# A two-block transformer kernel: attention probabilities scaled on ScalarE, chunks of a modulation product declared read one turn sooner, and weight copies placed ahead of waits

## The chip, the cores and the metric

The kernel runs on one core of a Trainium2 chip. The metric is the device time of one execution in microseconds (us); the time before is the median of three runs. A core has five engines that this text names: PE (TensorE, the matrix products), DVE (VectorE), ACT (ScalarE), POOL (GpSimd) and SP (SyncE, which here only issues transfers). Each engine works through its own list of instructions in order, and a semaphore holds one back until another engine has got far enough.

## The reference

What is computed is one token sequence of 256 rows by 1024 features that goes through a first block and then through two layers of a second kind, all in float32. Cut to what the change touches:

```python
# first block: m_lat = silu(c) @ w_ada + b_ada gives shifts, scales and gates
h = modulate(x, norm1_g, sh1, sc1)
z = h @ w_in + b_in                              # hyena input, q, k, v, gates
s_loc = einsum(q, k_window) * scale + rpb_bias   # 8 heads of 64, window over rows and columns
s_ctx = einsum(q, k_ctx) * scale
p = softmax(concat([s_loc, s_ctx]))              # 256 + 256 keys per query
y_na = (p @ [v_window; v_ctx]) @ w_na_out
y_hy = hyena(z) @ w_hy_out
x = x + g1 * ((sig_hy * y_hy + sig_na * y_na) @ w_out)
x = x + g2 * peer(modulate(x, norm2_g, sh2, sc2))
# then two layers
for l in range(2):
    a = dsa_attention(...)                       # 8 heads, softmax over 256 keys
    b = mamba2_branch(...)                       # state space product with decay exponentials
    x = x + (sigmoid(g_attn) * (a @ w_pa) + sigmoid(g_ssd) * (b @ w_ps)) @ w_o
    x = x + (silu(gate) * val) @ w_down          # gate, val = conv(rms_norm(x) @ w_up)
```

The modulation product `silu(c) @ w_ada` has one row only. Its later columns are computed not on PE but as dot products on DVE, from the transposed matrix `w_adaT`, of which each 512 KB chunk gives 128 of the columns.

## The kernel before, in words

**Products.** PE has no float32 product of full precision at full rate here; every product with weights is three products, w_hi·a_hi, w_lo·a_hi and w_hi·a_lo. ACT makes `w_hi` by copying a chunk out of the ring `wring` (L1440), POOL makes `w_lo` from it in two halves (L2809, L2811; for some matrices DVE does, L1876). The same is done with activations: ACT reads the high part from PSUM (`a_hi`, L1447) and DVE the low part (`a_lo`, L1953).

**The stream of weights.** SP issues the chunks in one fixed order, `wplan`, into a ring of six slots (L822 to L841). A chunk's transfer waits until the chunk six places ahead of it is no longer needed: for a product's chunk until its `w_lo` exists, for a chunk of `w_adaT` until its dot product has run. `weight_order` writes the plan and gives each chunk a turn, the place in the program at which the chunk is done with. The turns decide nothing about transfers; they decide where ACT, POOL and DVE put their copies in their own lists. `SplitStream.before(n)` issues every copy whose slot is done with by turn n, and it is called ahead of each wait for a filled bank (`wait_filled`), ahead of some reads (`wait_read`) and where `due` stands. `weights_upto` forces the copies up to a named chunk at once.

**The heads.** In the first block the eight attention heads go through a loop. For head h DVE adds the bias to the scores of two row tiles (L1960) and takes the maximum (L2259), adds the mask to the bias of the head after next (L1960), runs three modulation dots (`ada_dots`, L2241), takes the reciprocal of each row's sum (L2268) and multiplies the 128x512 exponentials by it (L2270), adds the gate bias in every other head (`gate_bias`, L2230), and at last writes the low part of the output of head h-1 (`na_low`, L1953). ACT takes the exponentials of head h with their sums (L1451), copies weights when they are due, reads the transposed probabilities of head h-1 out of PSUM (`nap`), and reads the high part of the output of head h-1 (`a_hi`, L1447). In the plan each head has two chunks of `w_in`, called W0 and W1 here, and then three of `w_adaT`, called A0, A1 and A2. With six slots and five chunks a head, W0 of head h+2 goes into the slot of A2 of head h, so its transfer waits until the last of the three dots of head h has run, and A0 of the next head waits until the `w_lo` of a W1 is made.

**Later places.** `exponentials` (L1730) is the softmax of the second block's attention, `decay` stands for the exponentials of the state space product (around L1785), `norm_tiles` and `tiles_turned` (L957) normalise and transpose the 256x1024 activations ahead of the feed-forward product.

## Time and profile before

| what | value |
|---|---|
| median of 3 runs | 2207.86 us (2206.05 to 2212.0) |
| profiled execution | 2212.09 us |
| its span | 2210.3 us |
| mean granted TensorE clock | 0.963 |
| PE busy | 1984.0 us, 90% of the span |
| DVE, ACT, POOL busy | 1377.4, 1002.8, 1048.6 us |
| memory read | 531.49 MB, 241 GB/s over the span |

The span runs from the first to the last instruction in the trace; what the profiled execution takes beyond it, 1.8 us, lies around it. PE at 90% says that most of the time a faster kernel would need less PE work or less waiting by PE; the places where PE is not busy are spread over few stages. The heads loop lies between 211 and 299 us, the second block begins past 1000 us, and its two layers repeat each other.

### The profile page before, as it was taken

The page shows a single profiled execution, that of the slowest core. Times are in us where ns is not written, and L with a number is a line of the kernel's source. Part 1 is how long each engine was busy: PE and PEld are TensorE (multiplying, and loading weights), DVE is VectorE, ACT ScalarE, POOL GpSimd, SP SyncE. Part 2 cuts the span into 40 slices and gives each one's busy share as a digit, 9 for nine tenths or more (in the row PEclk, how much of TensorE's full clock was granted, in tenths as well). Part 3 has the DMA queues.
Part 4 walks back from the last instruction along what each step waited for, and adds up shares of the span by engine and source line. Part 5 has one row for each costly group of instructions (what it writes and reads, how often), then busy time and mean ns, then how long its engine had stood idle before and what let it go on. Part 6 is the DMA issues. An engine that isn't in the chain of part 4 may idle for free.

```text
span 2210.3 us, 27141 instructions
## 1 busy us (share of the span) xinstructions
PE 1984.0 (90%) x9640; PEld 1469.2 (66%) x9640; DVE 1377.4 (62%) x2782; ACT 1002.8 (45%) x1836; POOL 1048.6 (47%) x840
## 2 busy tenths in 40 slices
PE   7999968987877787777999999999999999998998
PEld 1777756943323333333599777889989977777998
DVE  3768955486666676665457754167763775326776
ACT  1623435332222212212445687455564567845555
POOL 2362657764444444443387757900028865692000
PEclk9999979999898989999999999999999999999999
DMA  9242765699999999999655444545555534454553
GB/s 350 68 138 82 253 222 174 211 421 421 422 422 421 421 421 422 421 422 421 229 178 172 136 162 159 173 157 187 187 156 189 181 124 155 160 180 163 191 182 114
DMA packets 111447, 534.40 MB, mean 242 GB/s; under 512 B 12496, under 2 KB 12880, under 8 KB 77904
## 3 DMA queue, kind: packets, MB, share of 16 engines
q1 hardware_dynamic: 67104, 244.72, 33.1%
q0 software_dynamic: 38720, 275.96, 30.4%
q10 hardware_dynamic: 5488, 11.98, 1.7%
q8 instruction: 77, 1.26, 0.2%
q14 instruction: 58, 0.48, 0.1%
HBM read 531.49 MB, written 1.11 MB: 241 GB/s over the span
## 4 chain that ended last, share of the span: by engine, by line
PE 59%; DMA 22%; DVE 6%; ACT 6%; issue 3%; POOL 3%; ACTq 0%; POOLq 0%; DVEq 0%; SPq 0%
PE psum L877 57%; DMA pair_rows<-in_peer_uv,arena 11%; DMA arena<-in_peer_uv,arena 6%; DMA wring<-in_peer_uv,arena 3%; PE psum L945 2%; ACT w_hi L1440 2%; POOL w_lo L2811 2%; POOL w_lo L2809 1%; ACT arena L1451 1%; ACT arena L1785 1%; DVE arena L2551 1%; DMA wring<-in_w_in_hy 1%; DMA wring<-in_w_ada 0%; ACT arena L1730 0%; DVE arena L2567 0%
## 5 line engine op out<-in xcount | busy, mean ns | idle before, releaser
L2809 POOL TENSOR_TENSOR w_lo<-wring,w_hi 128x512 fp32r<-128x512 f32 x280 | 382.4, 1366 | 543.8 <-ACT w_hi L1440 535.5
L1440 ACT ACTIVATE w_hi<-wring 128x1024 fp32r<-128x1024 f32 (+1 forms) x414 | 433.7, 1054 | 334.4 <-PE psum L877 313.0
L877 PE MATMUL psum<-w_hi,a_hi 128*128 128x512 f32 (+1 forms) x1056 | 425.1, 403 | 44.8 <-POOL w_lo L2811 15.2
L877 PE MATMUL psum<-w_lo,a_hi 128*128 128x512 f32 (+1 forms) x1056 | 412.9, 391 | 0.0
L877 PE MATMUL psum<-w_hi,a_lo 128*128 128x512 f32 (+1 forms) x1056 | 412.3, 390 | 0.0
L877 PE MATMUL psum<-arena 128*128 128x512 f32 (+7 forms) x1142 | 336.3, 451 | 65.2 <-ACT arena L1658 50.7
L2811 POOL TENSOR_TENSOR w_lo<-wring,w_hi 128x512 fp32r<-128x512 f32 x280 | 394.8, 1410 | 0.0
L877 PE MATMUL psum<-a_hi,w_hi 128*128 128x256 f32 x1312 | 376.7, 287 | 4.1 <-DVE a_lo L1930 2.3
L877 PE MATMUL psum<-a_hi,w_lo 128*128 128x256 f32 x1312 | 372.0, 284 | 0.0
L877 PE MATMUL psum<-a_lo,w_hi 128*128 128x256 f32 x1312 | 371.9, 283 | 0.0
L877 PEld LDWEIGHTS psum<-arena 128*128 128x128 f32 (+2 forms) x1142 | 186.0, 198 | 198.0 <-issue 126.6
L877 PE MATMUL psum<-pair_rows,arena 128*128 128x512 f32 x512 | 247.2, 631 | 55.3 <-ACT arena L1658 55.3
L877 PEld LDWEIGHTS psum<-w_hi,a_hi 128*128 128x128 f32 x1056 | 201.4, 191 | 99.0 <-POOL w_lo L2811 18.0
L877 PEld LDWEIGHTS psum<-a_hi,w_hi 128*128 128x128 f32 x1312 | 252.2, 192 | 6.8 <-POOL w_lo L2811 3.0
L877 PEld LDWEIGHTS psum<-a_lo,w_hi 128*128 128x128 f32 x1312 | 252.5, 192 | 0.7
L877 PEld LDWEIGHTS psum<-a_hi,w_lo 128*128 128x128 f32 x1312 | 252.3, 192 | 0.0
L877 PEld LDWEIGHTS psum<-pair_rows,arena 128*128 128x128 f32 x512 | 100.4, 201 | 195.9 <-issue 118.0
L877 PEld LDWEIGHTS psum<-w_lo,a_hi 128*128 128x128 f32 x1056 | 201.7, 191 | 42.2 <-issue 3.9
L877 PEld LDWEIGHTS psum<-w_hi,a_lo 128*128 128x128 f32 x1056 | 201.4, 191 | 42.2
L2853 POOL DMA_INDIRECT pair_rows<-in_peer_uv,arena x128 | 137.3, 1072 | 162.8 <-PE psum L877 153.5
L1876 DVE TENSOR_TENSOR w_lo<-wring,w_hi 128x1024 fp32r<-128x1024 f32 x134 | 164.0, 1224 | 62.6 <-ACT w_hi L1440 59.1
L1653 ACT ACTIVATE arena<-arena 128x4 f32<-128x4 f32 (+2 forms) x69 | 14.3, 207 | 333.9 <-DVE arena L2428 333.9
(261 smaller groups left out, 2393.7 us busy)
## 6 DMA issues: line engine op xcount, KB each, us to landing
wring<-in_w_up SPq DMA_DIRECT2D x88, 512.0 KB, 3.3
wring<-in_w_xbc SPq DMA_DIRECT2D x48, 512.0 KB, 3.3
wring<-in_w_dn SPq DMA_DIRECT2D x44, 512.0 KB, 3.3
wring<-in_w_adaT SPq DMA_DIRECT2D x32, 512.0 KB, 4.3
wring<-in_w_qkv SPq DMA_DIRECT2D x32, 512.0 KB, 3.6
wring<-in_w_z SPq DMA_DIRECT2D x32, 512.0 KB, 3.2
wring<-in_w_g SPq DMA_DIRECT2D x32, 512.0 KB, 3.3
wring<-in_w_ps SPq DMA_DIRECT2D x32, 512.0 KB, 3.3
```

What stands on the lines that cost most here:

```text
L877: mm = lambda o, a, b, start, stop: nc.tensor.matmul(o, a, b, start=start, stop=stop, skip_group_check=True)
L945: m = nc.tensor.transpose(o[0:s.shape[-1], j * n:(j + 1) * n], s, ident[0:n, 0:n])
L1440: a.reaches(A(w_hi[:, n % SPLIT_RING, 0:width], wring[:, c % RING, 0:width], ACT.Copy), hi_ready, n + 1)
L1451: a.reaches(A(out_, in_, func, **kw), *read_value(name, i))
L1653: a.reaches(A(pact[:, cols_q], pdot[:, cols_q], ACT.Gelu), S("gelu_ready"), q + 1)
L1785: a.done(A(Lm[:, i % 2, (4 * half + j) * P:(4 * half + j + 1) * P], rows[:, j * P:(j + 1) * P], ACT.Relu, bias=acs_s[:, h:h + 1], scale=-1.0))
L1876: v.reaches(T.tensor_tensor(w_lo[:, r, 0:width], wring[:, c % RING, 0:width], w_hi[:, r, 0:width].bitcast(F32), ALU.subtract), *low_done(n))
L2551: ins = T.scalar_tensor_tensor(out=sc, in0=bank(L + "is", b_)[:, at * n_keys:(at + 1) * n_keys], scalar=wi[:, h:h + 1], in1=sc if h else c ...
L2809: nc.gpsimd.tensor_tensor(w_lo[:, r, 0:half], wring[:, c % RING, 0:half], w_hi[:, r, 0:half].bitcast(F32), ALU.subtract)
L2811: nc.gpsimd.tensor_tensor(w_lo[:, r, half:width], wring[:, c % RING, half:width], w_hi[:, r, half:width].bitcast(F32), ALU.subtract).then_ ...
L2853: pool.indirect_dma_start(out=pair(n), out_offset=None, in_=d["peer_uv"], in_offset=bass.IndirectOffsetOnAxis(ap=pidx[:, g, j:j + 1], axis ...
```

## The change

The change has five parts.

- The exponentials of a head are multiplied by the reciprocal of their sum on ACT (`Copy` with `scale=ainv`, sixteen of 128x512) and no longer on DVE. DVE makes the two reciprocals ahead of the three dots of the head, raises the new semaphore `na_inverse`, and has no multiplication left there. 
- In `weight_order` the turn of a `w_adaT` chunk of head h is `nao(h-1)` and no longer the turn after it.
- `tiles_turned` opens its eight PSUM banks one by one, each ahead of its first transpose, and not all eight ahead of the first.
- ACT's weight copies are forced earlier at four places: w_out 7 ahead of the first read of the output product, the second copy of `w2_z` ahead of the wait for the softmax maximum of the second row tile, `w2_o` 7 ahead of the reads of its product; and `w2_g` 5 moves to behind an `Exp`.
- POOL waits for `modulated_lo` and no longer for `tile_scaled` ahead of the low part of w_pq 1.

```diff
--- before.py
+++ after.py
@@ -381,7 +381,7 @@
             kp, c = 2 * ((h - 1) % 2) + k, (h - 1) // 2
             done = turn[("nap", 2 * h - 2)] if kp < 2 else turn[("gate", 2 * c)] if kp == 2 else turn[("gate", 2 * c + 1)] + 1
             w.append(("w_in", None, 12 + 4 * c + kp, CHUNK, done, kp == 3, True))
-        w.extend(("w_adaT", None, DOTS_PER_HEAD * (h - 1) + i, CHUNK, turn[("nao", h - 1)] + 1, True, False)
+        w.extend(("w_adaT", None, DOTS_PER_HEAD * (h - 1) + i, CHUNK, turn[("nao", h - 1)], True, False)
                  for i in range(DOTS_PER_HEAD))
     at = len(w)
     rows("w_hy_out", "mix", 2, two, 2)
@@ -949,9 +949,11 @@
 
         def tiles_turned(name, n):
 
-            o = [open_(name, k) for k in range(KD)]
+            o = []
             for t in range(TT):
                 for k in range(KD):
+                    if not t:
+                        o.append(open_(name, k))
                     if k % 4 == 0:
                         pe.wait_ge(S("tile_scaled"), 4 * n + 2 * t + k // 4 + 1)
                     m = nc.tensor.transpose(o[k][:, tile(t)], xs[:, t, tile(k)], ident)
@@ -1585,6 +1587,11 @@
                     read_out("nas", 2 * h + t, nap[h % 2][:, t, :], bank("nas", 2 * h + t), ACT.Exp,
                              bias=amax[:, 2 * h + t:2 * h + t + 1],
                              accum_out=asum[:, 2 * h + t:2 * h + t + 1])
+                for t in range(TT):
+                    i = 2 * h + t
+                    act.wait_ge(S("na_inverse"), i + 1)
+                    a.reaches(A(nap[h % 2][:, t, :], nap[h % 2][:, t, :], ACT.Copy, scale=ainv[:, i:i + 1]),
+                             S("na_prob"), i + 1)
             if h == 0:
                 act.wait_ge(S("c_row_in"), 16)
                 a.reaches(A(dve_junk[:], dve_junk[:], ACT.Silu), S("c_row_ready"), 1)
@@ -1604,6 +1611,8 @@
         for n in range(2):
             read_out("gb", n, G[:, 0, 512 * n:512 * n + 512], bank("gb", n))
         def first_half(i):
+            if i == 0:
+                weights_upto(act, "w_out", None, 7)
             due(act, "wout", i)
             wait_read(act, "wout", i)
 
@@ -1723,6 +1732,8 @@
 
             def exponentials(t, first):
                 n_keys = P * (t + 1)
+                if t:
+                    weights_upto(act, "w2_z", l, first + 1)
                 act.wait_ge(S("max2"), TT * l + t + 1)
                 for h in range(H2):
                     if h in (2, 5):
@@ -1787,10 +1798,12 @@
                     a.settle()
                     if i < SSD_G * TT - 1:
                         act.dma_start(rows, decay_rows(l, i + 1, half)).then_inc(S(f"decay_rows_in{half}"), 16)
-                    if i:
+                    if i and (i, half) != (1, 1):
                         ahead = 2 * i + 2 + half
                         weights_upto(act, *(("w2_g", l, ahead) if ahead < 16 else ("w2_pa", l, ahead - 16)))
                 a.reaches(A(Lm[:, i % 2, :], Lm[:, i % 2, :], ACT.Exp, scale=-1.0), S("decay_exp"), 8 * l + i + 1)
+                if i == 1:
+                    weights_upto(act, "w2_g", l, 5)
                 for g_ in range(SSD_G if i == 0 else 0):
                     read_out(L + "st", g_, st[:, g_, :], bank(L + "st", g_))
                 for n in (i - 1, i) if c else ():
@@ -1823,7 +1836,12 @@
                     weights_upto(act, *(("w2_o", l, 4) if k else ("w2_ps", l, 14)))
                 read_high(L + "mT", k, a_hi[:, k, :], bank(L + "mT", k)[:, 0:SEQ])
 
-            norm_tiles(1 + 2 * l, range(4), lambda i: wait_read(act, L + "wo", i))
+            def half_read(i):
+                if i == 0:
+                    weights_upto(act, "w2_o", l, 7)
+                wait_read(act, L + "wo", i)
+
+            norm_tiles(1 + 2 * l, range(4), half_read)
             scaled_high(L + "fT", KD, f"ffnw{l}")
             def glu_high(c):
                 for m_ in range(2):
@@ -2260,15 +2278,12 @@
                          S("na_max"), i + 1)
             if 0 < h < NA_HEADS - 1:
                 masked_bias(h + 1)
-            if h:
-                ada_dots(DOTS_PER_HEAD * (h - 1), DOTS_PER_HEAD * h)
             for t in range(TT):
                 i = 2 * h + t
                 wait_read(dve, "nas", i)
-                v.done(T.reciprocal(ainv[:, i:i + 1], asum[:, i:i + 1]))
-                v.settle()
-                v.reaches(T.tensor_scalar(nap[h % 2][:, t, :], nap[h % 2][:, t, :], ainv[:, i:i + 1], None, ALU.mult),
-                         S("na_prob"), i + 1)
+                v.reaches(T.reciprocal(ainv[:, i:i + 1], asum[:, i:i + 1]), S("na_inverse"), i + 1)
+            if h:
+                ada_dots(DOTS_PER_HEAD * (h - 1), DOTS_PER_HEAD * h)
             if h:
                 if h % 2 == 0:
                     gate_bias(h // 2 - 1)
@@ -2802,7 +2817,7 @@
             pool.wait_ge(hi_ready, n + 1)
             width, r = wplan[c][3], n % SPLIT_RING
             if c == chunk_at[("w_pq", None, 1)]:
-                pool.wait_ge(S("tile_scaled"), 4)
+                pool.wait_ge(S("modulated_lo"), 2 * KD + 1)
             if second_block + 2 <= c < second_block + SPLIT_RING:
                 pool.wait_ge(S("pair_used"), split_freed((SPLIT_RING + r) * CHUNK))
             half = width // 2
```

Rows of the engines' lists, as written out by the two programs. `w_hi<-wring` is a weight copy, and `weights_in2` the arrival of the chunk in ring slot 2. First ACT's list in the heads loop before, from the exponentials of one head:

```order
L1451 ACTIVATE arena,small_values<-psum,small_values 128x512 [waits psum_filled,na_max] x2
L1440 ACTIVATE w_hi<-wring 128x1024 [waits weights_used,weights_in2,psum_filled]
L1440 ACTIVATE w_hi<-wring 128x1024 [waits weights_used,weights_in3]
L1451 ACTIVATE arena<-psum 128x4x128 [waits psum_filled] x2
L1447 ACTIVATE a_hi<-psum 64x256 [waits psum_filled]
```

The same stretch of ACT's list after, from the reads of one head to those of the next:

```order
L1453 ACTIVATE arena<-psum 128x4x128 [waits psum_filled] x2
L1442 ACTIVATE w_hi<-wring 128x1024 [waits weights_used,weights_in2]
L1449 ACTIVATE a_hi<-psum 64x256 [waits psum_filled]
L1453 ACTIVATE arena,small_values<-psum,small_values 128x512 [waits psum_filled,na_max] x2
L1593 ACTIVATE arena<-arena,small_values 128x512 [waits na_inverse] x2
L1442 ACTIVATE w_hi<-wring 128x1024 [waits weights_used,weights_in3,psum_filled]
L1453 ACTIVATE arena<-psum 128x4x128 [waits psum_filled] x2
L1442 ACTIVATE w_hi<-wring 128x1024 [waits weights_used,weights_in1]
L1449 ACTIVATE a_hi<-psum 64x256 [waits psum_filled]
```

The copy of the slot 2 chunk (W0) has moved from behind the next head's exponentials to ahead of `a_hi` of this head, and there are two scalings behind the exponentials.

DVE's list in one head before, from the mask of the bias; ISA is the dot product and, with 128x1, the read of its sum:

```order
L1960 TENSOR_TENSOR arena<-arena 128x512 [waits rpb_in0]
L2241 ISA wring,small_values<-wring,dve_junk 128x1024 [waits weights_in0,c_row_ready]
L2241 ISA small_values 128x1
L2241 ISA wring,small_values<-wring,dve_junk 128x1024 [waits weights_in1]
L2241 ISA small_values 128x1
L2241 ISA wring,small_values<-wring,dve_junk 128x1024 [waits weights_in2]
L2241 ISA small_values 128x1
L2268 RECIPROCAL small_values<-small_values 128x1 [waits bank_read4]
L2270 TENSOR_SCALAR arena<-arena,small_values 128x512 [waits vector_steps]
L2268 RECIPROCAL small_values<-small_values 128x1 [waits bank_read5]
L2270 TENSOR_SCALAR arena<-arena,small_values 128x512 [waits vector_steps]
L1953 TENSOR_TENSOR a_lo<-psum,a_hi 64x256 [waits read_high,psum_filled]
```

The same head in DVE's list after:

```order
L1978 TENSOR_TENSOR arena<-arena 128x512 [waits rpb_in0]
L2284 RECIPROCAL small_values<-small_values 128x1 [waits bank_read4]
L2284 RECIPROCAL small_values<-small_values 128x1 [waits bank_read5]
L2259 ISA wring,small_values<-wring,dve_junk 128x1024 [waits weights_in0,c_row_ready]
L2259 ISA small_values 128x1
L2259 ISA wring,small_values<-wring,dve_junk 128x1024 [waits weights_in1]
L2259 ISA small_values 128x1
L2259 ISA wring,small_values<-wring,dve_junk 128x1024 [waits weights_in2]
L2259 ISA small_values 128x1
L1971 TENSOR_TENSOR a_lo<-psum,a_hi 64x256 [waits read_high,psum_filled]
```

The reciprocals, which wait for both exponentials (`bank_read4`, `bank_read5`), now stand ahead of the dots, and the two multiplications are gone.

## Rows read from the trace of the kernel before

**Rows 1.** the page: busy time by engine

```profile
PE 1984.0 (90%) x9640; PEld 1469.2 (66%) x9640; DVE 1377.4 (62%) x2782; ACT 1002.8 (45%) x1836; POOL 1048.6 (47%) x840
```

**Rows 2.** windows of two heads: PE, PEld, DVE, ACT, POOL busy; clock; DMA; GB/s

```profile
236.90:248.60 11.70, 11.70 (x49) 9.40 (x49) 10.45 (x16) 4.54 (x8) 7.17 (x5) 0.86 0.71 236
248.60:261.50 12.90, 10.49 (x50) 8.21 (x48) 11.71 (x19) 5.18 (x10) 8.31 (x6) 1.00 0.68 239
```

**Rows 3.** waits of PE, 211 to 299 us

```profile
PE psum L877 <- DVE arena L2230: 7.7, 3, 2.8
```

**Rows 4.** DVE in the heads: start, duration, instruction, count

```profile
224.76 0.41 DVE L1953 TENSOR_TENSOR a_lo<-psum,a_hi 64x256 fp32r<-64x256 f32 x1
...
249.41 0.42 DVE L1953 TENSOR_TENSOR a_lo<-psum,a_hi 64x256 fp32r<-64x256 f32 x1 [1.35 <-ACT a_hi L1447]
...
252.87 1.22 DVE L2241 CUSTOM_DVE_ANT_0 wring<-wring,dve_junk 128x1024 f32<-128x1024 f32 x1
...
255.15 2.28 DVE L2241 CUSTOM_DVE_ANT_0 wring<-wring,dve_junk 128x1024 f32<-128x1024 f32 x1
...
260.17 1.27 DVE L2230 TENSOR_TENSOR arena<-psum,arena 128x512 f32<-128x512 f32 x2
261.48 0.43 DVE L1953 TENSOR_TENSOR a_lo<-psum,a_hi 64x256 fp32r<-64x256 f32 x1
...
296.06 0.42 DVE L1953 TENSOR_TENSOR a_lo<-psum,a_hi 64x256 fp32r<-64x256 f32 x1 [1.20 <-ACT a_hi L1447]
```

**Rows 5.** ACT in the same head

```profile
248.93 0.38 ACT L1447 ACTIVATE a_hi<-psum 64x256 fp32r<-64x256 f32 x1 [3.20 <-PE psum L877]
...
252.97 0.19 ACT L1451 ACTIVATION_READ_ACCUMULATOR arena<-psum,small_values 128x1 f32 x1
253.06 1.99 ACT L1440 ACTIVATE w_hi<-wring 128x1024 fp32r<-128x1024 f32 x2
...
259.12 0.38 ACT L1447 ACTIVATE a_hi<-psum 64x256 fp32r<-64x256 f32 x1 [3.09 <-PE psum L877]
```

**Rows 6.** POOL in the same head

```profile
252.65 0.55 POOL L2823 DMA_DIRECT2D arena<-in_rpb  x1 [3.46 <-DVE small_values L2259]
254.20 2.15 POOL L2809 TENSOR_TENSOR w_lo<-wring,w_hi 128x512 fp32r<-128x512 f32 x1 [1.00 <-ACT w_hi L1440]
```

**Rows 7.** SP's queue: the transfers of W0 and W1 for head h+2

```profile
257.47 1.44 SPq L838 DMA_DIRECT2D wring<-in_w_in  x2
```

**Rows 8.** that transfer, and the first (222.04 us): size, us to landing

```profile
wring<-in_w_in SPq DMA_DIRECT2D x1, 512.0 KB, 3.7
...
wring<-in_w_in SPq DMA_DIRECT2D x1, 512.0 KB, 5.9
```

**Rows 9.** dots and multiplications: ns min/median/max, first and last start

```profile
L2241 DVE CUSTOM_DVE_ANT_0 wring<-wring,dve_junk x32: 1208/1222/2309, 218.5 to 351.6; 128x1024 f32<-128x1024 f32 x32
L2270 DVE TENSOR_SCALAR arena<-arena,small_values x16: 487/1294/1318, 214.0 to 293.6; 128x512 f32<-128x512 f32 x16
...
L1814 ACT ACTIVATE arena<-arena,small_values x16: 704/709/725, 1361.2 to 1930.1; 128x512 f32<-128x512 f32 x16
```

**Rows 10.** windows behind the last head

```profile
297.00:326.00 29.00, 13.96 (x58) 11.03 (x56) 13.48 (x21) 11.67 (x18) 18.59 (x12) 0.76 0.59 202
```

**Rows 11.** waits of PE, 1240 to 1300 us

```profile
PE psum L877 <- POOL w_lo L2811: 2.1, 1, 2.1
```

**Rows 12.** the window behind that wait

```profile
1260.00:1264.60 4.60, 4.60 (x14) 3.62 (x15) 2.08 (x1) 3.93 (x6) 4.25 (x3) 0.63 0.40 123
```

**Rows 13.** waits of PE at the feed-forward transposes, 1436 to 1456 us

```profile
PE psum L957 <- DVE arena L1904: 3.6, 1, 3.6
PE psum L877 <- POOL w_lo L2811: 1.1, 1, 1.1
```

**Rows 14.** DVE behind the modulated transposes of the first block

```profile
381.47 1.38 DVE L1930 TENSOR_TENSOR a_lo<-arena,a_hi 128x256 fp32r<-128x256 f32 x1
...
383.22 0.41 DVE L1930 TENSOR_TENSOR a_lo<-psum,a_hi 128x256 fp32r<-128x256 f32 x1
```

## The prediction

> **What bounds the kernel now.** I read the page's busy times first. PE is busy for 1984.0 of 2210.3 us [rows 1], so time can only go or come in the stages where PE waits. The windows show one such stage, the heads loop: one head takes 11.70 us with PE busy throughout at a granted clock of 0.86, the next 12.90 us with PE busy for 10.49 [rows 2]. The waits name the reason for the second kind: three stalls, 7.7 us together, on DVE's gate bias [rows 3]. That stall is no separate item. Read DVE's rows in order: the low part of a head's output, `a_lo`, starts at 249.41 and 261.48, and over six heads from 224.76 to 296.06 [rows 4]. (296.06 - 224.76) / 6 = 11.88 us is the period of the loop, and whatever makes DVE write `a_lo` later moves everything behind it, since the next head's score additions stand behind it on DVE.
>
> What lies in one period? From `a_lo` at 249.41, taken as zero: additions and maxima, the dots from +3.46 to +7.96 (252.87, then 1.15 apart, the third 2.28 long) [rows 4], two multiplications of 1.29 [rows 9] with their reciprocals, the gate bias at +10.76 and `a_lo` again at +12.07 [rows 4]. ACT has its exponentials' sums by +3.75, makes two weight copies in 1.99, and reads `a_hi` at 259.12, when PE has the product [rows 5]. SP issues W0 of head h+2 at 257.47, 0.1 after the last dot, because it goes into that dot's ring slot [rows 7]; it lands 3.7 us later, at 261.2 [rows 8]. Before, that landing is in nobody's way: the copy of W0 stands behind the next head's exponentials.
>
> **The change part by part.** *The new turn.* This edit is one number in `weight_order`, and it is the one that decides. The copy of W0 of head h+2 now stands in ACT's list ahead of `a_hi` of the same head. ACT is in order, so `a_hi` waits for the landing; DVE's `a_lo` waits for `a_hi`; the next head's additions, exponentials and dots wait for `a_lo`; and the next W0 is issued only behind those dots. The chain closes: dots, transfer, copy, `a_hi`, `a_lo`, additions, exponentials, dots. A transfer that was hidden becomes a link of the loop.
>
> *The reciprocals and multiplications.* Two multiplications leave DVE, 2 x 1.29 = 2.6 us a head [rows 9]. ACT's own scaling has no row; the nearest is its other 128x512 scaling from SBUF, 0.71 us [rows 9], so 1.4 a head, between 0.5 (what the quickest multiplication took on DVE) and 1.05 each (half of a double copy is 1.0 [rows 5]). ACT is idle for 3.09 us ahead of `a_hi` [rows 5], so this is hidden: nothing. In exchange the reciprocals now wait for both exponentials, whose sums are there at +3.75, so the first dot starts at about +3.95 in place of +3.46: +0.5. The gate bias (2.5 us) runs on DVE right behind the dots, while W0 is on its way (3.7 us), and costs nothing; its stall on PE is taken over by the wait for `a_hi`.
>
> *The new period.* Dots from +3.95, each 1.15 apart: end at +7.4. Then 0.1 issue, 3.7 landing, 1.0 copy and 0.4 for `a_hi` [rows 5, 7, 8]: 5.2. That makes 12.6 with three quick dots. A dot beside POOL's work takes 2.28 in place of 1.2 [rows 4], +1.1 each: 13.7, 14.8 and 15.9 with one, two and three slow ones. Before, only the third was slow, because POOL began its low part at 254.20, after ACT's copy, behind the bias transfer of 252.65 [rows 6]. Now W0's high part was made a head earlier, so POOL can begin at about +3.8, right behind that transfer and ahead of the first dot. I take two slow dots: 14.8. Six periods: (14.8 - 11.88) x 6 = +17.5; ends +4.3 and +24.1.
>
> The Trainium skill, "SBUF — State Buffer", section "Terms", says that DVE and GpSimd arbitrate for a port pair that is held exclusively for a whole instruction, the loser blocking. The lengths in rows 4 and 6 (a dot of 2.28, a low half of 2.15 against 1.37 on average) fit that rule; by it alone all three dots could alternate with POOL's halves, and the sum would take 15.9 for the period.
>
> *The first head.* The first W0 is issued at 222.04 and lands after 5.9 [rows 8]. With 0.5 for the reciprocals, 1.0 and 0.4, `a_lo` starts at 229.8 in place of 224.76 [rows 4]: +5.1.
>
> *Behind the last head.* From 297 to 326 PE is busy for 13.96 of 29 us and POOL for 18.59 [rows 10]: PE there waits for weight copies. One copy is already made when the loop ends, and transfers have had longer: I give back 4, between 0 and 8 (what two more chunks of copy and low part, 1.0 + 2.8 each, could be worth). The heads together: 17.5 + 5.1 - 4 = +18.6.
>
> *Copies ahead of waits.* At the second softmax of each layer PE stalls 2.1 us on a low part [rows 11], because ACT's copy for it stands behind the exponentials; the next 4.60 us run at a clock of 0.63, near the lower level of 1.2 GHz [rows 12], which costs about 4.60 x 0.37 = 1.7. The copy now stands ahead of that wait and pushes the exponentials by 1.0. I take 2.1 + 1.7 - 1.0 = 2.8 a layer, 5.6 for two; ends 0 (the softmax is late by as much) and 7.6. At the feed-forward transposes PE waits 1.1 for a low part [rows 13]; the earlier w2_o copy takes it: 2 x 1.1 = 2.2, ends 0 and 2.2. The 3.6 us wait of the transposes themselves is for DVE's data [rows 13], and opening banks one by one doesn't bring that sooner: nothing, at most some tenths. The copies of w_out 7 and w2_g 5 change places with neighbours while PE has work: nothing, within 1 either way.
>
> *POOL's wait.* The low part of w_pq 1 now begins after the modulated low parts; before, one of these was 1.38 long beside POOL and its like 0.41 [rows 14]: -0.9.
>
> **Sum.** +18.6 - 5.6 - 2.2 - 0.9 = +9.9 us. Against the profiled execution, 2212.1, that is 2222.0; the median of the runs is 4.2 lower than that execution, so the forecast is **2218**.
>
> **The rivals.**
> *One slow dot, as before.* The period is 13.7, (13.7 - 11.88) x 6 = +10.9, and the whole +10.9 + 5.1 - 4 - 8.7 = +3.3: 2211. For it: in before only one of three was slow. Against: POOL's low part is ready sooner. 0.2.
> *The full alternation of dots and halves* (the reading that the page's rule gives): 15.9, +24.1 + 5.1 - 4 - 8.7 = +16.5: 2224. For it: the lengths fit. Against: POOL has four halves of some 1.4 to do, and the bias transfer ahead of them. 0.15.
> *The late copies give nothing,* since the softmax or the data is late anyway: +18.6 - 0.9 = +17.7: 2226. For it: PE's wait on DVE of 3.6 right beside the 1.1 [rows 13]. 0.1.
> *The other side: PE bounds the heads.* In the head from 236.90, PE was busy to the end [rows 2] and ACT read `a_hi` at 248.93, when PE had it [rows 5]. If W0 lands by the time PE has the head's product, the copy ahead of `a_hi` costs 1.0 at most, and with 2.6 us off DVE the loop goes at PE's pace, 10.5 a head: (11.88 - 10.5) x 6 = -8.3, with the late copies -17: 2191. It decides from the point where the last dot ends 5.2 us ahead of that product. For it: the 2.6 us are real. Against: the dots start later, not sooner, and the sum from +3.95 to `a_lo` has no PE in it. 0.1.
> The main case has 0.45; its own range is 2213 to 2223.
>
> **How the numbers follow.** A measurement of this kernel can tell 0.3%, 6.6 us, from no change: the bounds are 2201 and 2214.5. Slower: of the main case 0.37, the full alternation 0.15, no gain later 0.1: 0.62. Same: 0.08 of the main case and 0.17 of the one slow dot: 0.25. Faster: PE's pace 0.1 and 0.03 of the one slow dot: 0.13. The range 2203 to 2228 leaves out PE's pace and the far end of the two dear cases.
>
> **What would show it.** The period of `a_lo` on DVE between the second and the eighth head: near 14.8 if right, 12 or less if the loop argument is wrong. ACT's weight copy ahead of `a_hi` should have idle time ahead of it that ends with a transfer of w_in, some 2 to 3 us in each head, and `a_hi` none that ends with PE. Two of three dots should be 2 us or longer. PE's stall on the gate bias should be gone and a longer one, on `a_lo` or `a_hi`, stand in its place. At the second softmax the stall on POOL's low part should be gone with the clock at full level behind it. If W0 is found landed before the copy gets to it in most heads, the forecast is wrong.

## The result, and the profile after

The changed kernel takes 2243.94 us (median of 4 runs, 2243.19 to 2244.54); the kernel before, beside it, 2207.63. The ratio is 1.0161, 95% interval 1.0143 to 1.0179: 36 us slower. The forecast was 2218, with a range that ended at 2228. The direction and the loop were as foretold; what one turn of the loop costs was not.

The profiled execution's span is 2242.7 us against 2210.3, 32.4 more. The page has the same number of matmuls, 18.8 us more of PE busy time and none more on DVE. The mean granted clock is 0.953 and was 0.963; in the six turns of the heads it lies between 0.65 and 0.96, before between 0.85 and 1.00, and the 0.65 belongs to the turn from 268.87 on, just ahead of which PE had waited 4.7 us. So part of the loss shows as longer matmuls, the rest, 13.6 us, as idle time of PE:

```profile
PE 2002.8 (89%) x9640; PEld 1482.2 (66%) x9640; DVE 1377.2 (61%) x2766; ACT 1012.0 (45%) x1852; POOL 1032.0 (46%) x840
```

The same matmul can be found in both traces, since PE's order is the same but for where banks are opened; the difference of its two starts says how late the changed kernel is at that point. First the changed kernel's PE at the output product of the first block and at the first product behind the modulated transposes; the instructions answering to them in the kernel before start at 326.29 and 382.99:

```profile
361.70 0.76 PE L877 MATMUL psum<-w_hi,a_hi 128*128 128x512 f32 x1 [11.31 <-DVE arena L2309]
...
417.35 0.55 PE L877 MATMUL psum<-a_hi,w_hi 128*128 128x256 f32 x1 [0.78 <-DVE a_lo L1948]
```

| stretch | forecast | measured in the traces |
|---|---|---|
| ahead of the heads | 0 | +1.1 |
| first head (to the first `a_lo`, 232.08 against 224.76) | +5.1 | +6.2 |
| six periods | +17.5 | +34.2 |
| last heads to the output product | -4 | -6.1 |
| behind the modulated transposes | -0.9 | -1.1 |
| all later stages | -7.8 | -1.9 |
| sum | +9.9 | +32.4 |

The sum is 32.4 and not 36 because the profiled execution of the kernel before was 4.5 us above its median and that of the changed kernel 0.6. The +1.1 ahead of the heads has arisen before 100 us, where nothing was edited; at that point the profiled executions of the twelve runs lie between 0.0 and 3.6 us behind the kernel before. Differences of that size between two whole traces can't be put down to an edit.

Now one turn of the loop. DVE, with the columns start, duration, instruction, count (the rows answer to [rows 4]):

```profile
232.08 0.42 DVE L1971 TENSOR_TENSOR a_lo<-psum,a_hi 64x256 fp32r<-64x256 f32 x1 [5.15 <-ACT a_hi L1449]
...
250.34 0.43 DVE L1971 TENSOR_TENSOR a_lo<-psum,a_hi 64x256 fp32r<-64x256 f32 x1 [4.90 <-ACT a_hi L1449]
...
254.26 5.95 DVE L2259 CUSTOM_DVE_ANT_0 wring<-wring,dve_junk 128x1024 f32<-128x1024 f32 x1
...
260.14 1.22 DVE L2259 CUSTOM_DVE_ANT_0 wring<-wring,dve_junk 128x1024 f32<-128x1024 f32 x1
...
261.28 1.21 DVE L2259 CUSTOM_DVE_ANT_0 wring<-wring,dve_junk 128x1024 f32<-128x1024 f32 x1
...
268.87 0.42 DVE L1971 TENSOR_TENSOR a_lo<-psum,a_hi 64x256 fp32r<-64x256 f32 x1 [6.36 <-ACT a_hi L1449]
...
337.61 0.42 DVE L1971 TENSOR_TENSOR a_lo<-psum,a_hi 64x256 fp32r<-64x256 f32 x1 [7.21 <-ACT a_hi L1449]
```

(337.61 - 232.08) / 6 = 17.59 us is the period, and the turn shown takes 18.53, against 11.88 before and 14.8 in the forecast. The dots run from +3.92 to +12.15 and no longer to +8.0, and it is the first of them that is long. POOL in that stretch answers to [rows 6]:

```profile
253.59 0.55 POOL L2838 DMA_DIRECT2D arena<-in_rpb  x1 [12.74 <-DVE small_values L2277]
254.16 1.29 POOL L2824 TENSOR_TENSOR w_lo<-wring,w_hi 128x512 fp32r<-128x512 f32 x1
255.39 1.29 POOL L2826 TENSOR_TENSOR w_lo<-wring,w_hi 128x512 fp32r<-128x512 f32 x1
256.63 1.27 POOL L2824 TENSOR_TENSOR w_lo<-wring,w_hi 128x512 fp32r<-128x512 f32 x1
257.85 1.27 POOL L2826 TENSOR_TENSOR w_lo<-wring,w_hi 128x512 fp32r<-128x512 f32 x1
```

The first dot starts 0.1 us behind the first of four low halves, and ends 1.1 us behind the last of them. The halves themselves are at their quick length of 1.27 to 1.29. SP and ACT then show the transfer and what waits for it (to [rows 5, 7]):

```profile
260.24 1.47 SPq L838 DMA_DIRECT2D wring<-in_w_adaT  x2
262.53 0.80 SPq L838 DMA_DIRECT2D wring<-in_w_in  x2
```

```profile
267.44 1.06 ACT L1442 ACTIVATE w_hi<-wring 128x1024 fp32r<-128x1024 f32 x1 [10.19 <-DMA wring<-in_w_in]
268.40 0.36 ACT L1449 ACTIVATE a_hi<-psum 64x256 fp32r<-64x256 f32 x1
```

W0 is issued as the last dot ends, ACT's copy starts 4.91 us later (the landing took 3.7 before [rows 8]), and the copy ahead of `a_hi` has waited 10.19 us. ACT's waits over all heads, in total, times and longest, name the transfer six times:

```profile
ACT w_hi L1442 <- DMA wring<-in_w_in: 53.1, 6, 10.3
```

The dots and the scalings on ACT, in ns (to [rows 9]): the scaling costs what its neighbour led one to expect, 0.71, and the longest dot 5.95.

```profile
L2259 DVE CUSTOM_DVE_ANT_0 wring<-wring,dve_junk x32: 1211/1226/5950, 222.3 to 386.9; 128x1024 f32<-128x1024 f32 x32
L1593 ACT ACTIVATE arena<-arena,small_values x16: 705/714/717, 215.7 to 326.2; 128x512 f32<-128x512 f32 x16
```

### The profile page after: what moved, and what is told of

Same layout as the page of the kernel before. It is cut to its first block, busy times and chain, and to the rows that moved or that the text cites. A ratio compares the mean times of both kernels' runs of the same rounds, so it can differ in the third digit from the quotient of the medians.

```text
span 2242.7 us, 27135 instructions
## 1 busy us (share of the span) xinstructions
PE 2002.8 (89%) x9640; PEld 1482.2 (66%) x9640; DVE 1377.2 (61%) x2766; ACT 1012.0 (45%) x1852; POOL 1032.0 (46%) x840
## 4 chain that ended last, share of the span: by engine, by line
PE 57%; DMA 23%; DVE 8%; ACT 6%; issue 4%; POOL 2%; ACTq 0%; DVEq 0%; SPq 0%; another core or an unknown queue 0%; POOLq 0%
PE psum L877 55%; DMA arena<-in_peer_uv,arena 8%; DMA pair_rows<-in_peer_uv,arena 7%; DMA wring<-in_peer_uv,arena 4%; DVE wring L2259 2%; ACT w_hi L1442 1%; PE psum L945 1%; DMA wring<-in_w_in 1%; ACT arena L1453 1%; POOL w_lo L2826 1%; POOL w_lo L2824 1%; DMA wring<-in_w_in_hy 1%; DVE arena L2566 1%; ACT arena L1796 0%; DVE arena L2582 0%
## 5 line engine op out<-in xcount | busy, mean ns | idle before, releaser
L2824 POOL TENSOR_TENSOR w_lo<-wring,w_hi 128x512 fp32r<-128x512 f32 x280 | 373.1, 1332 | 558.7 <-ACT w_hi L1442 548.5
L877 PE MATMUL psum<-arena 128*128 128x512 f32 (+7 forms) x1142 | 351.7, 466 | 72.7 <-ACT arena L1667 49.7
L2826 POOL TENSOR_TENSOR w_lo<-wring,w_hi 128x512 fp32r<-128x512 f32 x280 | 387.3, 1383 | 0.0
L877 PEld LDWEIGHTS psum<-arena 128*128 128x128 f32 (+2 forms) x1142 | 192.5, 204 | 210.6 <-issue 124.3
L877 PE MATMUL psum<-pair_rows,arena 128*128 128x512 f32 x512 | 251.9, 642 | 62.1 <-ACT arena L1667 62.1
```

What stands on the lines that cost most here:

```text
L877: mm = lambda o, a, b, start, stop: nc.tensor.matmul(o, a, b, start=start, stop=stop, skip_group_check=True)
L2824: nc.gpsimd.tensor_tensor(w_lo[:, r, 0:half], wring[:, c % RING, 0:half], w_hi[:, r, 0:half].bitcast(F32), ALU.subtract)
L2826: nc.gpsimd.tensor_tensor(w_lo[:, r, half:width], wring[:, c % RING, half:width], w_hi[:, r, half:width].bitcast(F32), ALU.subtract).then_ ...
```

## The experiments

There are twelve runs; e11 is the kernel of e1 once more and e12 the changed kernel. The medians of the kernel before, beside them, lie between 2209.9 and 2211.9 us, since they ran on other occasions than the first comparison; so the ratios are compared.

| kernel | median us | ratio to before (95%) | mean period, six heads |
|---|---|---|---|
| before | 2207.63 | 1 | 11.88 |
| changed | 2243.94 | 1.0161 (1.0143 to 1.0179) | 17.59 |
| e1, turn put back | 2201.64 | 0.9960 (0.9944 to 0.9976) | 10.71 |
| e2, turn alone | 2237.11 | 1.0119 (1.0095 to 1.0144) | 16.82 |
| e3, low part ahead of the bias | 2225.90 | 1.0071 (1.0048 to 1.0095) | 14.52 |
| e4, scaling alone | 2207.64 | 0.9982 (0.9970 to 0.9994) | 10.74 |
| e5, late edits alone | 2210.60 | 0.9993 (0.9983 to 1.0003) | 11.89 |
| e6, copy behind `a_hi` | 2220.09 | 1.0036 (1.0024 to 1.0047) | 12.91 |
| e7, gap between halves | 2236.26 | 1.0114 (1.0096 to 1.0132) | 15.38 |
| e8, W0 transferred alone | 2239.74 | 1.0126 (1.0108 to 1.0145) | 16.65 |
| e9, e1 with POOL gated | 2200.86 | 0.9951 (0.9931 to 0.9971) | |
| e10, e1 without the w2_z copy | 2200.70 | 0.9949 (0.9932 to 0.9967) | |
| e11, e1 again | 2204.77 | 0.9971 (0.9958 to 0.9985) | |
| e12, changed again | 2242.91 | 1.0150 (1.0130 to 1.0170) | 17.52 |

**e1: is it the turn?**

```diff
-        w.extend(("w_adaT", None, DOTS_PER_HEAD * (h - 1) + i, CHUNK, turn[("nao", h - 1)], True, False)
+        w.extend(("w_adaT", None, DOTS_PER_HEAD * (h - 1) + i, CHUNK, turn[("nao", h - 1)] + 1, True, False)
```

> The changed kernel with the turn of the w_adaT chunks put back by one, so that ACT copies W0 of head h+2 behind the next head's exponentials again; all else of the change stays. Theory (the copy ahead of a_hi closes the loop over the transfer): the period of a_lo falls from 17.6 us to 12 or less, the heads lose all of their +35 us, and the later stages keep their gain of some 4 us: 2195 to 2206 us, at or below the kernel before. Rival (the new place of reciprocals and multiplications is at fault, since the first dot starts behind both exponentials): the time stays above 2225 us, and first dots of 5.9 us are still there.

The whole loss goes with this one number, and the rest of the change is a gain of 0.4% (0.3% in e11). The period is 10.5 us in five heads of six. PE's window over one of them (columns as in [rows 2]) shows 10.3 of 10.5 busy at a granted clock of 1.00, and ACT's read of `a_hi` waits for PE again:

```profile
242.18:252.63 10.45, 10.32 (x50) 8.28 (x49) 8.06 (x14) 6.03 (x11) 6.60 (x6) 1.00 0.84 277
```

```profile
252.15 0.38 ACT L1449 ACTIVATE a_hi<-psum 64x256 fp32r<-64x256 f32 x1 [2.11 <-PE psum L877]
```

This is the pace of PE that one of the rivals had named, 10.5 a head. The rival's road to it (the transfer lands in time although the copy stands ahead of `a_hi`) did not come about in any run.

**e2: is the turn enough alone?** On the kernel before:

```diff
-turn[("nao", h - 1)] + 1, True, False)
+turn[("nao", h - 1)], True, False)
```

> The kernel before with only the turn of the w_adaT chunks lowered by one. Theory: the loop over the transfer is there in full without any of the other edits: a period of 16 to 18.5 us, the heads longer by 25 to 38 us, 2233 to 2246 us, and ACT's copy of W0 waits for the transfer in each head. The same goes for the rival that the moved multiplications matter, turned round: then this kernel is within 8 us of the one before, 2200 to 2216 us.

It is: 1.0119, with first dots of 6.4 us in four heads, and ACT's copies wait for the transfer as long as in the changed kernel:

```profile
ACT w_hi L1440 <- DMA wring<-in_w_in: 54.9, 6, 11.6
```

**e3: does the first dot wait for POOL's four halves?**

```diff
             if h >= 2:
                 due(pool, "nas", 2 * (h - 2) + 1)
+                if h >= 4:
+                    ahead = streams[id(pool)]
+                    ahead.upto(split_chunks[ahead.n])
                 pool.wait_ge(S("na_max"), 2 * (h - 2) + 2)
             pool.dma_start(nabias[h % 2], d["rpb"][h]).then_inc(S(f"rpb_in{h % 2}"), 16)
```

> The changed kernel, but for heads 4 to 7 POOL makes the low part of W0 ahead of the transfer of the position bias, and so does not meet the first dot with four halves in a row. Theory (a dot that meets POOL's halves back to back waits for all four): the first dots of 5.95 us become 1.2 us, one of three dots is 2.3 us, as in the last two heads, the period of those four heads falls from 18.6 to about 15.5, and the time by 4 x 3.0 = 12 us, to 2230 to 2234 us. Rival (the first dot is long for another reason, as the arrival of its chunk or of the bias): the dots stay at 5.9 us and the time within 4 us of 2244.

All four long dots are gone, no dot in the heads is longer than 2.28 us, and the time falls by 18 us, more than the 12 expected. POOL makes W0's low part while DVE writes `a_lo`, and the bias transfer finds POOL idle; DVE's first dot is quick:

```profile
249.40 1.27 POOL L2824 TENSOR_TENSOR w_lo<-wring,w_hi 128x512 fp32r<-128x512 f32 x1 [5.76 <-ACT w_hi L1442]
...
253.09 0.55 POOL L2841 DMA_DIRECT2D arena<-in_rpb  x1 [1.20 <-DVE small_values L2277]
```

```profile
249.84 0.43 DVE L1971 TENSOR_TENSOR a_lo<-psum,a_hi 64x256 fp32r<-64x256 f32 x1 [6.11 <-ACT a_hi L1449]
...
253.75 1.22 DVE L2259 CUSTOM_DVE_ANT_0 wring<-wring,dve_junk 128x1024 f32<-128x1024 f32 x1
```

With the collision taken out the period is 14.52, close to the 14.8 of the forecast, but not by its terms: one dot of three is slow and not two, and the copy of W0 starts 3.5 to 5.7 us after the issue and not 3.7. The ratio 1.0071 is a loss of 16 us.

**e4: the scaling on ACT and the reciprocals ahead of the dots, alone**, on the kernel before; ACT's part:

```diff
+                for t in range(TT):
+                    i = 2 * h + t
+                    act.wait_ge(S("na_inverse"), i + 1)
+                    a.reaches(A(nap[h % 2][:, t, :], nap[h % 2][:, t, :], ACT.Copy, scale=ainv[:, i:i + 1]),
+                             S("na_prob"), i + 1)
```

DVE's part is the two moved reciprocals and the two multiplications less, as in the change.

> The kernel before with only the multiplications moved to ACT and the two reciprocals ahead of the dots. Theory (two multiplications of 1.3 us leave DVE, but PE is close behind in the heads without a gate bias): the period falls from 11.9 by 0.3 to 1.2 us, 2200 to 2207 us. Rival (the dots start later, so the transfers and all that follows come later): 2 to 6 us slower, 2210 to 2214 us.

The period falls to 10.74, 6.9 us over six heads, and the kernel gains 0.18%, 4 us. Part of the gain is lost in the first head, whose dots now wait for both exponentials: its first dot starts at 221.78, before at 218.49, and `a_lo` at 228.78, before at 224.76; 0.5 of each was there ahead of the heads. In the later heads the first dot starts 0.5 later, and the shorter period shows that this costs nothing there.

**e5: everything but the heads.** This is e1 with e4's part taken back:

```diff
-                    a.reaches(A(nap[h % 2][:, t, :], nap[h % 2][:, t, :], ACT.Copy, scale=ainv[:, i:i + 1]),
-                             S("na_prob"), i + 1)
...
+                v.reaches(T.tensor_scalar(nap[h % 2][:, t, :], nap[h % 2][:, t, :], ainv[:, i:i + 1], None, ALU.mult),
+                         S("na_prob"), i + 1)
```

> Everything of the change but the heads: turn, multiplications and reciprocals are as before; the copies ahead of waits, the banks opened one by one and POOL's wait stay. Theory: these are the 6 us by which the kernel with the turn back lies below the one with the multiplications alone, so 4 to 8 us faster than before; the stall on POOL's low part at both second softmaxes is gone. Rival (they gain nothing alone, the late stages differed by chance): within 2 us of before.

0.9993, with an interval that holds 1: as a whole these edits can't be told from nothing, and my 4 to 8 us were wrong. The interval reaches from 4 us of gain to 1 of loss, so it doesn't rule out the 2 to 3 us that the traces show at the feed-forward product (see the last part on the prediction). Where most of the gain went is told with e9.

**e6: the copy one instruction later**, on e1:

```diff
             if h >= 1:
                 na_turned(h - 1)
+            if 1 <= h < NA_HEADS - 1:
+                ahead = streams[id(act)]
+                ahead.upto(split_chunks[ahead.n])
```

> The kernel with the turn back, but ACT copies W0 of head h+2 right behind a_hi, where it has idle time before the next exponentials. Theory (the same copy one instruction later): a_hi does not wait for the transfer; W0 lands 3.7 us behind the last dot, about 1 to 2 us ahead of the next exponentials, so the copy is nearly hidden. But POOL then has W0's low part to do behind the bias transfer, in a row with W1's, and the first dot waits for four halves again: a period of 13 to 15 us, 2215 to 2228 us. Rival (the collision needs the late chain of the changed kernel): a period of 10.5, within 3 us of the kernel with the turn back.

The forecast of slower held, with the time inside its range and the period of 12.91 just below: `a_hi` waits for PE again (3.20 us), but the exponentials of the next head now stand behind the transfer, and dots of up to 5.86 us are back. First and second dot of one head on DVE, and POOL beside the first:

```profile
259.97 2.88 DVE L2262 CUSTOM_DVE_ANT_0 wring<-wring,dve_junk 128x1024 f32<-128x1024 f32 x1
...
262.78 2.28 DVE L2262 CUSTOM_DVE_ANT_0 wring<-wring,dve_junk 128x1024 f32<-128x1024 f32 x1
```

```profile
260.48 1.28 POOL L2829 TENSOR_TENSOR w_lo<-wring,w_hi 128x512 fp32r<-128x512 f32 x1
262.07 1.91 POOL L2827 TENSOR_TENSOR w_lo<-wring,w_hi 128x512 fp32r<-128x512 f32 x1 [0.31 <-ACT w_hi L1442]
```

The first dot waits for two halves (the first of them starts at 259.23), POOL's queue is empty for 0.31 us, and the dot comes in; the next half then takes 1.91.

Against e1, whose only difference is the place of six copies, this is 0.76% slower. An early copy is not free even where its own engine is idle. Two prices are mixed here: the copy waits for its transfer, up to 7.25 us, with the exponentials behind it, and POOL begins early, beside the dots. How much each costs isn't shown.

**e7: a gap between the halves.**

```diff
+            if c in gap_before:
+                pool.wait_ge(S("ada_dots"), gap_before[c])
             half = width // 2
...
+        gap_before = {chunk_at[("w_in", None, 12 + 2 * h + 1)]: DOTS_PER_HEAD * (h - 1) + 1 for h in range(2, 6)}
```

> The changed kernel, but in the four heads with a long first dot POOL begins the low part of W1 only when the first dot is done; W0's two halves stay where they are. Theory (a dot waits for as many halves as stand in a row): the first dot takes 5.95 - 2 x 1.26 = 3.4 us, the later ones meet W1's halves (one of 2.3), the dots end 1.2 to 2.5 us sooner, the period falls to 16 to 17.4 and the time by 5 to 10 us, to 2234 to 2239 us. Rival (the length of the first dot has nothing to do with the number of halves): 5.9 us stay, and the time is 2244 us or above.

POOL first, then DVE:

```profile
252.48 1.28 POOL L2826 TENSOR_TENSOR w_lo<-wring,w_hi 128x512 fp32r<-128x512 f32 x1
253.71 1.27 POOL L2828 TENSOR_TENSOR w_lo<-wring,w_hi 128x512 fp32r<-128x512 f32 x1
256.23 2.14 POOL L2826 TENSOR_TENSOR w_lo<-wring,w_hi 128x512 fp32r<-128x512 f32 x1 [1.24 <-DVE small_values L2259]
```

```profile
252.57 3.50 DVE L2259 CUSTOM_DVE_ANT_0 wring<-wring,dve_junk 128x1024 f32<-128x1024 f32 x1
```

With two halves in a row in place of four the first dot takes 3.50 in place of 5.95, which is two halves of 1.23 less. So the first dot of a head, when it starts just behind a half, has waited for every half that followed without a break, and in e6 0.31 us of break let it in. By the medians 8 us of the time come back.

This doesn't hold for every dot. In e1 the third dot meets POOL, and starts 0.17 us behind the first of four halves that follow one another without a break (the last two start at 251.77 and 253.02). It waited for one half only, and the second half waited for it:

```profile
248.40 2.29 DVE L2259 CUSTOM_DVE_ANT_0 wring<-wring,dve_junk 128x1024 f32<-128x1024 f32 x1
```

```profile
248.23 1.38 POOL L2824 TENSOR_TENSOR w_lo<-wring,w_hi 128x512 fp32r<-128x512 f32 x1 [2.24 <-ACT w_hi L1442]
249.56 2.25 POOL L2826 TENSOR_TENSOR w_lo<-wring,w_hi 128x512 fp32r<-128x512 f32 x1
```

And in e2 the first dot starts, by its record, 0.36 us ahead of POOL's first half, right behind POOL's bias transfer, and still ends only 1.1 us behind the fourth half:

```profile
253.22 6.39 DVE L2241 CUSTOM_DVE_ANT_0 wring<-wring,dve_junk 128x1024 f32<-128x1024 f32 x1
```

```profile
253.00 0.56 POOL L2823 DMA_DIRECT2D arena<-in_rpb  x1 [13.73 <-DVE small_values L2259]
253.58 1.28 POOL L2809 TENSOR_TENSOR w_lo<-wring,w_hi 128x512 fp32r<-128x512 f32 x1
```

So neither who starts first nor how much POOL has queued decides alone whether the two take turns. In e1 the dot before was still running when the half began, and in e2, e7 and the changed kernel there was no dot before; whether that is the reason, no run tests.

**e8: the landing.**

```diff
+            if name == "w_in" and i >= 12 and i % 2:
+                sp.wait_ge(weights_in[(c - 1) % RING], 16 * ((c - 1) // RING + 1))
             src = d[name][i] if l is None else d[name][l, i]
```

> The changed kernel, but SP issues W1 of each head, and with it all that stands behind, only when W0 has landed. Theory (the landing of W0 takes 4.5 to 5.1 us here in place of 3.7 since W1 and A0 are issued right behind it and share the memory): W0 lands in 3.5 to 4 us, the period falls by about 1 us, the time by 4 to 8 us, to 2236 to 2240, if the later chunks are not late. Rival (the landing is longer because of the chunks A1 and A2 issued ahead of it): W0 takes 4.5 us or more still, and the time stays at 2244 or rises.

SP issues W1 only when W0 has landed. The time falls by 4 us, the period of the four slow heads from 18.6 to 18.1, and W0 is copied 4.1 to 4.6 us after its issue there, against 4.5 to 5.1 in the changed kernel. But the interval overlaps that of e12, the changed kernel once more, which has 4.5 to 5.9 from the second head on. And e7, where W1 and A0 are issued as close behind W0, has 3.5 to 4.3. So that the transfers behind W0 make its landing longer isn't shown; the cause is open. In e7 W0 is issued 2.2 us behind the transfer ahead of it, in the slow heads of the changed kernel and of e8 1.15 us; but the changed kernel's W0 of 314.85, issued 2.2 us behind too, was copied only after 5.5.

> The changed kernel once more, unchanged, for a second look at two numbers of its profile. Theory: the four first dots of 5.95 us are fixed by the order of POOL's halves and are there again to the tenth; the landing of W0 (4.5 to 5.5 us in its first profile, 3.5 to 4.6 with three of its relatives) belongs to the memory's state in that execution as much as to the kernel, and may come out between 3.5 and 5.5. The time is 2240 to 2246 us. Rival (the long landing is fixed by the order of the transfers): the same 4.5 to 5.5 in every head.

There the four first dots are 5.92 to 5.94 us again.

**e9, e10 and e11: the second softmax.** In the changed kernel PE's wait of 2.1 us on POOL's low part [rows 11] is gone, but another of 2.0 has come ahead of it:

```profile
1286.36 0.38 PE L877 MATMUL psum<-small_values,consts 128*128 128x32 f32 x2 [2.01 <-DVE a_lo L1971]
```

DVE just before, and POOL beside it:

```profile
1282.68 1.22 DVE L1985 SCALAR_TENSOR_TENSOR dve_junk<-dve_junk,small_values 128x64 f32<-128x64 f32 x1
1283.93 1.16 DVE L1982 TENSOR_SCALAR dve_junk<-dve_junk 128x64 f32<-128x64 f32 x1
...
1285.53 1.28 DVE L1971 TENSOR_TENSOR a_lo<-psum,a_hi 128x512 fp32r<-128x512 f32 x2
```

```profile
1282.56 1.26 POOL L2824 TENSOR_TENSOR w_lo<-wring,w_hi 128x512 fp32r<-128x512 f32 x1 [0.24 <-ACT w_hi L1442]
1283.78 1.27 POOL L2826 TENSOR_TENSOR w_lo<-wring,w_hi 128x512 fp32r<-128x512 f32 x1
```

The early copy lets POOL make its halves at 1282.56, beside a chain of small vector operations (the softplus of the state space product). Two of them take 1.22 and 1.16 us. The same two in the kernel before, where POOL was idle, take 0.2:

```profile
1246.92 0.22 DVE L1967 SCALAR_TENSOR_TENSOR dve_junk<-dve_junk,small_values 128x64 f32<-128x64 f32 x1
1247.18 0.19 DVE L1964 TENSOR_SCALAR dve_junk<-dve_junk 128x64 f32<-128x64 f32 x1
```

Behind them stands `a_lo`, and PE waits for it. One stall was turned into another of the same length, in both layers. In e9 POOL waits until that chain is through; in e10 the copy goes back behind the exponentials; e11 is e1 once more, to compare with.

```diff
+            if wplan[c][:3] in gated:
+                pool.wait_ge(S("adt_ready"), wplan[c][1] + 1)
             half = width // 2
...
+        gated = {("w2_z", l, 15) for l in range(LAYERS)}
```

> The kernel with the turn back, but POOL begins the low part of the w2_z chunk that ACT now copies early only when DVE's chain of small vectors (softplus for the state space product) is through. Theory (the late copy gives its gain back because POOL's two halves meet that chain and hold a_lo up by 2 us, for which PE then waits): the 2.0 us wait of PE on a_lo ahead of the second softmax goes in both layers, the wait on POOL's low part stays gone, and the time falls by 2 x 2 = 4 us against the kernel with the turn back, to 2195 to 2200 us. Rival (the softmax is late by as much anyway): the wait moves on to another place and the time is within 2 us of the kernel with the turn back.

```diff
-                if t:
-                    weights_upto(act, "w2_z", l, first + 1)
```

> The kernel with the turn back, and the copy of w2_z back behind the exponentials; the other late copies stay. Theory: the stall of 2.1 us on POOL's low part is there again, that of 2.0 on a_lo gone, and only the lower clock behind it (1.7 a layer) tells them apart: 1 to 4 us slower than the kernel with the turn back, 2202 to 2206. Rival (the early copy as it stands is worth nothing at all): within 1 us of it.

> The kernel with the turn back once more, beside the two others on the same chip, to compare with: 2199 to 2204 us, 0.4% below the kernel before.

e9 has neither stall in either layer. DVE's small operations are back at 0.2 (the second, at 1241.40, takes 0.20) and POOL begins behind them:

```profile
1241.14 0.23 DVE L1985 SCALAR_TENSOR_TENSOR dve_junk<-dve_junk,small_values 128x64 f32<-128x64 f32 x1
```

```profile
1242.26 1.27 POOL L2826 TENSOR_TENSOR w_lo<-wring,w_hi 128x512 fp32r<-128x512 f32 x1 [1.49 <-DVE small_values L2648]
```

Its span is 2196.0 us, the shortest of the profiled executions, and between matching matmuls around the softmax it is 2.5 us a layer shorter than e1. But its median, 2200.86, is level with e10's 2200.70, where the stall of 2.1 on POOL's low part is back in both layers, and both intervals overlap that of e11. e9 came out 4 us below e11, as forecast, though just above its range; e10 was forecast 1 to 4 us slower than the kernel with the turn back, with a rival of no difference; it came out 4 us below e11, which neither foresaw, and e11 itself, 0.3% below before, lies just above its forecast. So the early copy as the change has it is worth nothing that can be measured, perhaps it costs a little; that the gated one is better than none is seen in the trace only, and not settled by the times. The change without its new turn is 0.3 to 0.5% faster than before in all four sets of runs (e1, e9, e10, e11), and which of the three kernels is best isn't settled.

## Why the prediction was wrong

*The new turn closes the loop over the transfer.* Right, and shown: e1 takes the whole loss away with that one number, and e2 brings 27 us with it alone. The copy waits for the transfer in all six heads, `a_hi` no longer for PE.

*The length of the dots.* This is the step that failed: "A dot beside POOL's work takes 2.28 in place of 1.2 [rows 4], +1.1 each", and "I take two slow dots: 14.8". I had seen what matters, that POOL could begin right behind the bias transfer, ahead of the first dot, and then priced a meeting of the two as it stood in the trace of before, where they took turns. There POOL met the last dots of a head, and each waited for one instruction of the other. Here four halves stand ready in a row right behind the bias transfer when the first dot of the head comes, and the dot waits for all of them: 5.95 us in place of 2.28. Only the first dot was slow, and not two. The dots end at +12.15 and not +9.6, which is 2.6 us a head in four heads. e3 and e7 show it from two sides. Even the rival of "full alternation", 15.9, rested on a fair exchange that no row had promised for this order. The rule of the Trainium skill, "SBUF — State Buffer", section "Terms" (an exclusive lock, the loser blocking fully), fits the rows in which dots and halves take turns (2.28 and 2.25). It doesn't say who is next when the holder has more work queued: in the rows of e6 and e7 the dot came in where POOL's queue had a break, in those of e1 without one. And the dot of e2, which by its record started ahead of the first half and yet was held, isn't explained by it.

*The landing.* I took 3.7, from one row; the copy started 4.5 to 5.5 us after the issue from the second head on, 1.2 more in the turn shown. Why it was longer is open after e8. A range from 3.7 to the first transfer's 5.9 [rows 8] would have held it.

*The two together.* 2.6 and 1.2 make 3.8 on 14.8: 18.6; the four heads had 18.3 to 18.8. The last two, where POOL has no bias transfer to hold it back, had 15.6 and 15.7.

*The first head* was +6.2 for +5.1, but by luck: W0 was issued at 226.96, which, without the 1.1 from ahead of the heads, is 3.3 later than the 222.04 + 0.5 of the forecast, since all three dots waited for the exponentials there and the third was slow; and its copy started 3.7 later and not 5.9. *The tail* was -6.1 for -4, *POOL's wait for w_pq 1* -1.1 for -0.9: the low part of 1.38 us [rows 14] is a quick one now,

```profile
416.79 0.41 DVE L1948 TENSOR_TENSOR a_lo<-arena,a_hi 128x256 fp32r<-128x256 f32 x1
```

*The reciprocals and multiplications* were to cost nothing on ACT: right. That PE's stall on the gate bias would be taken over by the wait for `a_hi` was half right: PE still waits for the gate bias, 7.5 us in two waits where it had been 7.7 in three [rows 3], and 7.8 us in two for `a_lo` besides (211 to 340 us):

```profile
PE psum L945 <- DVE a_lo L1971: 7.8, 2, 4.7
PE psum L877 <- DVE arena L2248: 7.5, 2, 4.4
```

What I did not credit is what they give once the loop is open: 1.1 us a head (e4), down to PE's pace.

*The signs.* The copy ahead of `a_hi` was to be idle for 2 to 3 us, and was for 5.3 to 10.3; that too says that the loop had been read rightly and its length had not.

*The late copies*, -7.8, were -1.9 in the traces and nothing certain in the times (e5). Of the -5.6 for the second softmax about -1 is left. The step "pushes the exponentials by 1.0" looked for the price on the engine that copies. It was paid on DVE, by POOL's halves that the copy set free. The -2.2 for the feed-forward product was right: the wait of 1.1 ahead of the transposes [rows 13] is gone in both layers. From the matmul behind a wait of 0.7 on `a_lo`, which both kernels have, to the transposes it was 21.55 us before and is 20.19:

```profile
1429.42 0.47 PE L877 MATMUL psum<-w_hi,a_hi 128*128 128x512 f32 x1 [0.72 <-DVE a_lo L1953]
...
1450.97 2.84 PE L957 MATMUL psum<-consts,arena 128*128 128x128 f32 x16 [3.60 <-DVE arena L1904]
```

```profile
1464.28 0.47 PE L877 MATMUL psum<-w_hi,a_hi 128*128 128x512 f32 x1 [0.72 <-DVE a_lo L1971]
...
1484.47 3.65 PE L959 MATMUL psum<-consts,arena 128*128 128x128 f32 x16 [3.60 <-DVE arena L1922]
```

The second layer has 21.53 and 20.18, so the two together gave 2.7. The remaining +1.8 of the later stages arises elsewhere; between 383 and 1100 us, where nothing was edited, the two traces drift apart and together again by as much as 4 us. The 3.6 of the transposes themselves is what it was. Opening banks one by one thus did nothing, as forecast.

## What to carry to other kernels

In a chain of engines that work in order, ask of each copy that is moved up not only what it waits for but whether its wait lies on a loop: a transfer that is issued at the end of the same loop wasn't hidden any more here. And follow the copy one engine further: what it makes ready early starts early, next to other work than before. Where two engines block each other, a length read where they took turns isn't the price of every meeting: with work queued on one side the first dot here paid for all of it, 5.95 us for 2.28.

## What the runs showed of the hardware

A DVE dot of 128x1024 with two SBUF operands, 1.22 us alone, took 5.95 us when it was the first of its head and started 0.1 us behind the first of four POOL subtractions of 128x512 that followed each other without a break, and 3.50 with two of them. It took 2.28 where the two engines took turns, in e1 also with four subtractions in a row. In e2 it took 6.39 although its record starts 0.36 us ahead of the first subtraction. POOL's halves kept 1.25 to 1.30 us while a first dot waited, and took 2.1 to 2.3 where they waited for a dot. Even small DVE operations of 128x64 between SBUF tiles went from 0.2 to 1.2 us beside a half. DVE's `a_lo` of 128x256 took 1.38 us beside POOL with both operands in SBUF, 0.41 without POOL. A 512 KB transfer of weights in the heads was copied 3.5 to 5.9 us after its issue, and in two runs of one kernel the same transfer differed by up to 1.2 us.
